# A loop of its own for the memory attention: new order of turns, scores, rounding, outputs and filling products

## What is computed

```python
def memory_cross_attention(u, mem_n, w_mq, w_mkv, w_mo):
    q = (u @ w_mq).reshape(B, S, MEM_HEADS, MEM_HEAD_DIM)        # 4 heads of 256
    k, v = jnp.split(mem_n @ w_mkv, 2, axis=-1)                  # 256 memory tokens
    s = jnp.einsum('bshd,bnhd->bhsn', q, k) * (MEM_HEAD_DIM ** -0.5)
    p = jax.nn.softmax(s, axis=-1)
    o = jnp.einsum('bhsn,bnhd->bshd', p, v).reshape(B, S, D_MODEL)
    return o @ w_mo
```

## Time and profile before

| what | value |
|---|---|
| three runs, median | 1203.12 us |
| the profiled execution | 1202.4 us |
| its span, first to last instruction | 1200.7 us |
| TensorE matmuls busy | 1162.8 us (97% of the span), x5565 |
| VectorE, ScalarE, GpSimd busy | 355.6, 445.9, 472.7 us |
| mean granted clock of TensorE | 0.994 |
| first scores of the memory attention | 724.06 us |
| first matmul behind the last head's outputs | 790.07 us |

### The profile page before, as it was taken

How to read it: one execution, slowest core, us unless ns; L and a number is a source line. 1 busy time by engine, 2 the same in 40 slices (tenths; PEclk the granted TensorE clock), 3 DMA queues, 4 the chain that set the end, 5 groups by cost and what they waited for, 6 DMA issues and landing times.

```text
span 1200.7 us, 14983 instructions
## 1 busy us (share of the span) xinstructions
PE 1162.8 (97%) x5565; PEld 963.0 (80%) x5565; DVE 355.6 (30%) x713; ACT 445.9 (37%) x728; POOL 472.7 (39%) x216
## 2 busy tenths in 40 slices
PE   8999999999999999999899999799999999999998
PEld 6888888888888778788678878678888888888886
DVE  3131221310006264655546104516213122130003
ACT  5232232322126455454535534425523223232213
POOL 2344354354442542222224753122543434435441
PEclk9999999999999999999999999899999999999999
DMA  6232323232322222111223442022332333323233
GB/s 197 88 105 87 105 87 105 88 105 88 105 90 69 88 88 71 53 53 54 71 70 117 146 142 88 18 71 71 93 101 94 98 97 95 100 93 104 90 102 109
DMA packets 83835, 110.91 MB, mean 92 GB/s; under 512 B 8718, under 2 KB 53836, under 8 KB 83788
## 3 DMA queue, kind: packets, MB, share of 16 engines
q1 hardware_dynamic: 83696, 110.24, 28.1%
q10 hardware_dynamic: 92, 0.02, 0.0%
HBM read 108.14 MB, written 2.10 MB: 92 GB/s over the span
## 4 chain that ended last, share of the span: by engine, by line
PE 67%; issue 19%; POOL 8%; DVE 4%; ACT 1%; DMA 1%; SPq 0%; POOLq 0%; DVEq 0%; ACTq 0%
PE bank L1397 22%; PE bank L1401 22%; PE bank L1398 22%; POOL w_lo L566 7%; DVE h L1050 1%; DVE tmp L1039 1%; DMA raw<-in_ffn_w_gu 1%; ACT w_hi L622 0%; POOL q_hi L604 0%; POOL q_lo L604 0%; DVE pt_lo L1170 0%; DVE xl L1002 0%; PE bank L1418 0%; PE bank L1421 0%; DVE smax L1144 0%
## 5 line engine op out<-in xcount | busy, mean ns | idle before, releaser
L566 POOL TENSOR_TENSOR w_lo<-raw,w_hi 128x1024 fp32r<-128x1024 f32 x193 | 461.5, 2403 | 707.5 <-ACT w_hi L622 695.2
L1397 PE MATMUL bank<-xh,w_hi 128*128 128x512 f32 (+1 forms) x920 | 353.3, 384 | 5.2 <-POOL w_lo L566 2.6
L1401 PE MATMUL bank<-xl,w_hi 128*128 128x512 f32 (+1 forms) x920 | 351.8, 382 | 0.0
L1398 PE MATMUL bank<-xh,w_lo 128*128 128x512 f32 (+1 forms) x920 | 351.7, 382 | 0.0
L622 ACT ACTIVATE w_hi<-raw 128x1024 fp32r<-128x1024 f32 x196 | 204.5, 1056 | 361.3 <-DMA raw<-in_ffn_w_down 169.3
L1397 PEld LDWEIGHTS bank<-xh,w_hi 128*128 128x128 f32 x920 | 173.0, 188 | 40.3 <-issue 3.9
L1401 PEld LDWEIGHTS bank<-xl,w_hi 128*128 128x128 f32 x920 | 173.1, 188 | 33.9
L1398 PEld LDWEIGHTS bank<-xh,w_lo 128*128 128x128 f32 x920 | 173.2, 188 | 32.2
L1397 PE MATMUL bank<-w_hi,mid_hi 128*128 128x512 f32 x352 | 137.3, 390 | 0.0
L1398 PE MATMUL bank<-w_hi,mid_lo 128*128 128x512 f32 x352 | 137.0, 389 | 0.0
L1401 PE MATMUL bank<-w_lo,mid_hi 128*128 128x512 f32 x352 | 137.0, 389 | 0.0
(11 more groups left out here) (227 smaller groups left out, 1168.6 us busy)
## 6 DMA issues: line engine op xcount, KB each, us to landing
raw<-in_ffn_w_gu SPq DMA_DIRECT2D x176, 256.0 KB, 2.9
raw<-in_ffn_w_down SPq DMA_DIRECT2D x88, 256.0 KB, 2.8
raw<-in_mix_w_in SPq DMA_DIRECT2D x48, 256.0 KB, 2.8
raw<-in_mem_w_kv SPq DMA_DIRECT2D x32, 256.0 KB, 3.1
raw<-in_mix_w_out SPq DMA_DIRECT2D x16, 256.0 KB, 2.8
raw<-in_mem_w_q SPq DMA_DIRECT2D x16, 256.0 KB, 3.0
raw<-in_mem_w_o SPq DMA_DIRECT2D x16, 256.0 KB, 2.9
h<-in_x SPq DMA_DIRECT2D x4, 512.0 KB, 5.3
```

Of the source, the lines that this page charges most:

```text
L566: gp.tensor_tensor(w_lo[:, n % SLOTS, :], raw[:, n % SLOTS, :], w_hi[:, n % SLOTS, :].bitcast(F32), ALU.subtract).then_inc(lo_ready, 1)
L1397: pe.matmul(dst, w[0], x[0], start=start, stop=False, skip_group_check=loose)
L1398: pe.matmul(dst, w[1], x[0], start=False, stop=False, skip_group_check=loose)
L1401: return pe.matmul(dst, w[0], x[1], start=False, stop=stop, skip_group_check=loose)
```

## The change

The loops for FoX and for the memory attention are parted on ScalarE and VectorE (`fox_attention`, `mem_attention`) and on TensorE. FoX's order stays as it was. In the memory attention:

- TensorE turns unit k-2 first in the iteration, ahead of the filling and of `scores(k)`. A head's outputs come in iteration k for unit k-2 (before: for k-3), so there are 18 iterations, and the first two quarters still stand before the first scores.
- ScalarE rounds unit k-2's turned rows ahead of exponential k. `round_to` moves to the end of the iteration, behind the output copies. The two output copies have the copy-out of the query chunks between them.
- VectorE makes unit k-2's low part first, then maximum k, `normalise(k-1)`, and the output copies. `mq_lo` stands in the same iteration as `mq_hi` (before: one later).
- The filling ends one iteration earlier: three quarters in iterations 3 and 4, one in iterations 6 and 7. The first pair of chunks is complete in iteration 5 (before: 6), the last in iteration 7 (before: 8).

```diff
-EARLY_OUT = ((0,), (1,), ())
+EARLY_OUT = ((0,), (1,))
-MEM_FILL = ((2, 0), (1, 1), (1, 1), (1, 1), (1, 1), (1, 1), (1, 1), (0, 1), (0, 1))
+MEM_FILL = ((2, 0), (1, 1), (1, 1), (1, 2), (1, 2), (1, 1), (0, 1), (0, 1))
...
             def mem_attention():          # ScalarE
...
+                for k in range(N_MEM + LATE):
+                    if k >= LATE:
+                        turned_hi(k - LATE)
+                    if k < N_MEM:
+                        exponent(k)
+                    ended = k >= LATE and MEM_UNITS[k - LATE][1] == TC - 1
+                    if ended:
+                        output(MEM_UNITS[k - LATE][0], 0)
+                    if k == MEM_PAIR_TURN:
+                        mq_hi(1, (0, 1))
+                    if ended:
+                        output(MEM_UNITS[k - LATE][0], 1)
+                    if k == len(MEM_FILL) - 1:
+                        mq_hi(1, (2, 3))
+                    round_to(mem_block("q", 1, 0) + 3 + MEM_FILLED[min(k, len(MEM_FILL))] // 4
+                             + (k > len(MEM_FILL)))
...
             def mem_attention():          # VectorE
...
+                for k in range(N_MEM + LATE):
+                    if k >= LATE:
+                        turned_lo(MEM, k - LATE)
+                    if k < N_MEM:
+                        dve.wait_ge(scored, u + 1)
...                                        # maximum, scaled maximum: as before
+                    if 1 <= k <= N_MEM:
+                        normalise(N_FOX + k - 1, NMEM)
+                    if ended:
+                        output(MEM_UNITS[k - LATE][0], 0)
+                    if k == MEM_PAIR_TURN:
+                        mq_lo(1, (0, 1))
+                    if ended:
+                        output(MEM_UNITS[k - LATE][0], 1)
+                    if k == len(MEM_FILL) - 1:
+                        mq_lo(1, (2, 3))
...
-                for k in range(len(units) + late + 1):          # TensorE
-                    mem_fill(filled, before)
-                    scores(k)
-                    first_output(EARLY_OUT[k - len(units)])
-                    output(k - late - 1, 0)
-                    mem_fill(filled + before, after)
-                    output(k - late - 1, 1)
-                    turn(k - late)
+                    for k in range(N_MEM + LATE):
+                        if k >= LATE:
+                            turn(k - LATE)
+                        mem_fill(filled, before)
+                        if k < N_MEM:
+                            scores(k)
+                        else:
+                            first_output(EARLY_OUT[k - N_MEM])
+                        output(k - LATE, 0)
+                        mem_fill(filled + before, after)
+                        output(k - LATE, 1)
```

More of the change, by code:

```diff
@@ L804, in cum_spread, with fox_attention @@
                 act.activation(cum_b[:, hd % 2, :], bank[cum_slot(hd) % 2][:, :], ACT.Copy).then_inc(cb_ready, 1)
-            def attention(phase):
-                units, u0, late, mem = UNITS[phase], FIRST_UNIT[phase], LATE, phase != FOX
+            def fox_attention():
                 def output(done):
-                    if not 0 <= done < len(units) or units[done][1] < TC - 1:
+                    if not 0 <= done < N_FOX or FOX_UNITS[done][1] < TC - 1:
                         return
[L813 to L824, removed]
-                        cum_spread(k // TC + 1)
[L826 to L840, removed]
-                        round_to(B_IN + KB * FILL_GROUPS[0] + 2 + sum(FILL[:k]) // 4)
[L842 to L854, removed]
-                                       ACT.Copy).then_inc(pt_h, 1)
[L856 to L867, removed]
@@ L935, in mixer @@
                 in_evacuate(2, (2, 3))
-                attention(FOX)
+                fox_attention()
                 gla()
@@ L964, in memory @@
                 act.wait_ge(hinv, 3)
-                attention(MEM)
+                mem_attention()
                 round_to(B_UP2)
@@ L1137, in attention @@
-                for k in range(len(units) + late + 2):
-                    if k < len(units):
-                        u, w = u0 + k, key_width(mem, units[k][1])
+                    hd = FOX_UNITS[done][0]
+                    r = slice(FOX_D * (hd % 2), FOX_D * (hd % 2 + 1))
+                    dve.wait_ge(y_h, hd + 1)
+                    dve.tensor_tensor(fox_lo[r, hd // 2, :], o_bank(FOX, hd)[r, :], fox_hi[r, hd // 2, :].bitcast(F32),
+                                      ALU.subtract).then_inc(y_l, 1)
@@ new lines, in fox_attention @@
+                for k in range(N_FOX + LATE + 2):
+                    if k < N_FOX:
+                        hd, i = FOX_UNITS[k]
+                        w, r = key_width(False, i), slice(k % 4, k % 4 + 1)
+                        dve.wait_ge(scored, k + 1)
+                        if i == 0:
+                            dve.wait_ge(cb_ready, hd + 1)
+                        if k >= PROBS:
+                            dve.wait_ge(pturned, k - PROBS + 1)
+                        dve.tensor_tensor_reduce(prob[:, k % PROBS, 0:w], s_bank(FOX, k)[:, 0:w],
+                                                 cum_b[:, hd % 2, 0:w], -1.0, -NEG, ALU.add, ALU.min,
+                                                 accum_out=nmx[:, r]).then_inc(maxed, 1)
+                    if 1 <= k <= N_FOX:
+                        normalise(k - 1, key_width(False, FOX_UNITS[k - 1][1]))
+                    if k == 0:
+                        in_evacuate(2, (2, 3))
+                    if k == 2:
+                        in_evacuate(1, (), (2, 3))
+                    if 0 <= k - LATE < N_FOX:
+                        turned_lo(FOX, k - LATE)
+                    output(k - LATE - 1)
+                    for g in (3, 5):
+                        if k == PAIR_TURN[g - 3]:
+                            in_evacuate(g, (0, 1))
+                        if k == END_TURN[g - 3]:
+                            in_evacuate(g, (2, 3))
+                    if 0 < k - END_TURN[0] <= 3:
+                        decayed(k - END_TURN[0] - 1)
@@ L1158, in attention @@
[L1158 to L1168, removed]
-                        dve.wait_ge(pt_h, u0 + k - late + 1)
-                        dve.tensor_tensor(pt_lo[:, js, i * P:(i + 1) * P],
-                                          p_bank(phase, k - late)[:, 0:nk * P].rearrange("p (j n) -> p j n", n=P),
-                                          pt_hi[:, js, i * P:(i + 1) * P].bitcast(F32),
-                                          ALU.subtract).then_inc(pt_l, 1)
@@ L1698, in output @@
                     last.then_inc(pv_done, 1)
-                for k in range(len(units) + late + 1):
-                    before, after = MEM_FILL[k] if mem and k < len(MEM_FILL) else (0, 0)
-                    filled = MEM_FILLED[k] if k < len(MEM_FILL) else 0
-                    mem_fill(filled, before)
-                    if k < len(units):
-                        scores(k)
-                    if phase == FOX:
-                        fill(k)
-                    if mem and k >= len(units):
-                        first_output(EARLY_OUT[k - len(units)])
-                    output(k - late - 1, 0)
-                    mem_fill(filled + before, after)
-                    if mem:
-                        output(k - late - 1, 1)
-                    if 0 <= k - late < len(units):
-                        turn(k - late)
+                if mem:
+                    for k in range(N_MEM + LATE):
+                        before, after = MEM_FILL[k] if k < len(MEM_FILL) else (0, 0)
+                        filled = MEM_FILLED[k] if k < len(MEM_FILL) else 0
+                        if k >= LATE:
[8 more added lines that the diff above has]
+                        output(k - LATE, 1)
+                    return
+                for k in range(N_FOX + LATE + 1):
+                    if k < N_FOX:
+                        scores(k)
+                    fill(k)
+                    output(k - LATE - 1, 0)
+                    if 0 <= k - LATE < N_FOX:
+                        turn(k - LATE)
             def first_output(ms):
```

121 lines of the change are left out of this document (76 added, 45 removed).

## The result

The changed kernel is slower: 1210.32 us in the median of 4 runs (1209.93 to 1211.19) against 1203.18 us before; ratio 1.0057, 95% interval [1.0041, 1.0073]. I had forecast 1205.0 us in a range of 1199.8 to 1208.2, "no change" with 0.67; the third rival, slower through half clock, said 1208.5. The forecast was wrong. Of all launches reported here one, of e2_psum_exp, took 3014 us, at a granted clock of 1.0; it is left out of that kernel's median and interval.

What follows compares the result with a forecast made beforehand. TensorE, busy 97% of the span, was taken to bound the kernel, so only its stalls and slow clock could go. Order +0.3 and half clock +2.1 gave +2.4 us on 1202.4: 1204.8, stated as 1205.0, range 1199.8 to 1208.2.

Steps and rivals of the forecast that it cites:

- no change: Whole kernel: a measured time within about 0.3%, 3.6 us, of the time before; chance 0.67.
- the third rival: Between 767 and 787, thinly filled iterations pull the clock down again and again: +6.1 us, 1208.5; chance 0.16.
- The order, iteration by iteration: Memory attention, worked through to head 3's outputs: at full clock throughout, the change ends 0.3 us later.
- behind an output copy: Iteration 14: the output copy stands in front of the high part, without rounding; the iteration takes 2.95 us.
- over two outputs: Iteration 13: 1.38 us to the output and 2.84 for both outputs, 4.22 us in all.
- stalls before turns 5, 7 and 9: TensorE waits before turning units 5, 7 and 9, in iterations 7, 9 and 11: 1.3, 2.6 and 2.6 us.
- wait for query chunks: The 2.5 us wait before scores 8 goes in name; its copies still hold up the turn.
- The clock: Memory attention: half clock behind the two 2.6 us stalls, before iterations 9 and 11, costs 2.1 us.
- Two stretches of half clock: Outputs of head 1, 1.4 to 1.6 us, and the plain iteration 11, whose scores are delayed by 0.7.
- its upper bound: Four remaining stretches between 771 and 787 at half clock too: 0.7 for three plain ones, 1.6 for outputs, 3.7 us more.
- Rival 2: Memory attention: the new loop doesn't bind, turns stay 2.00 us apart; -4.2 us, 1198.5; chance 0.14.
- The signs that I had named: Wrong if TensorE's stalls sum under 8 or over 18 us, iteration 5 waits for GpSimd's split, or stage end moves outside 0-5 us.

Runs made afterwards that it cites:

- e2_psum_exp: The changed kernel with the memory attention's exponentials left in their PSUM bank, so VectorE's normalising reads PSUM and writes SBUF; median 1209.21 us.
- e3: The changed kernel with TensorE's turn of unit k-2 put behind the scores of k, except where it closes a head; median 1206.78 us.
- e4: The changed kernel with roundings moved on ScalarE: blocks 0 and 1 behind exponential 4, block 2 behind 9, block 3 behind 13; median 1205.14 us.

## Why the prediction was wrong

- **The order, iteration by iteration: right.** At held clock the stage is 65.05 us; the working gave 787.56 - 724.06 = 63.5, and with the 1.62 us of the port 65.1. Turns at 2.42 and 2.41 (said 2.43), 2.94 behind an output copy (2.95), 4.23 over two outputs (4.22). The stage after has the stalls before turns 5, 7 and 9 (1.9, 2.4, 3.3 us; said 1.3, 2.6, 2.6), and the wait for query chunks is gone in name, as said.
- **The clock: mis-sized, and this is the step that failed.** "I take 2.1 us": it was 4.9. Two stretches of half clock were allowed for, on the outputs of head 1 (1.4) and on iteration 11 (0.7); the trace has 0.52 and 0.59 us there. The stretches behind them, between 771 and 787, I put at nothing in the sum, though I had named them as its upper bound. They took 0.76 us in iteration 12, 1.49 in 13 and 1.56 in 16, 3.8 us in all. The 3.7 us that I had named for them is what came, but the range did not reach that far. I treated the clock as a matter of single long stalls. Over the plain iterations, with stalls of 1.2 us between short groups of matmuls, it stayed down for 10 us. That was the third rival (0.16), and its test, a clock below 0.8 over 765:785, is met with 0.74. Its 1208.5 is 1.8 us short, about the long rows of the next point. In reading the kernel before I had also counted three shorter stalls behind the 2.15 us one that left the clock alone; the trace has four (0.93, 0.79, 1.75 and 1.13 us).
- **The port: missing.** 1.62 us stood in none of the terms. The sum of 0.33 + 1.62 + 4.92 us gives 6.87 of the 6.91 measured. Neither miss alone would have left the range: 1205.0 with the 2.8 us of clock is 1207.8, with the 1.6 us of the port 1206.6, with both 1209.4. In the memory attention of the kernel before the same instruction was never above 0.45 us, because its roundings stood where the splits missed it or met it only in their last 0.3 us; moving `round_to` moved the splits onto it. I had followed `round_to` through ScalarE's queue, and asked of GpSimd only whether the weights came in time.
- **Rival 2 was right about what is possible, not about this kernel**: in the changed kernel it takes VectorE's low part behind the normalising for turns to come under 2.1 us apart (1.37).
- **The signs that I had named.** One sign of being wrong came: the first matmul behind the last head's outputs starts at 797.58 us, 7.5 us later than before, where I had allowed 0 to 5. TensorE's stalls of 13.1 us lie within 8 to 18, and no wait for GpSimd's split appeared.
- What stays open: why half clock fell on one stretch rather than another in kernels with like stalls (e2, e3, e4). The runs show that it goes when TensorE is kept at work, in three pairs of kernels: the stage of the profiled executions falls by 5.0, 4.1 and 2.4 us, the medians against their own before by 3.2, 4.6 and 2.9.

## What to carry to other kernels

When two queues hand work back and forth, write the loop with its lags: an operation that needs this iteration's product, put first in its queue, makes everything behind it wait, while last in its queue it has an iteration of slack. A moved instruction moves what it releases: look at what runs beside the released work, on shared ports too. Where thin iterations follow one another, price half clock over the whole stretch and not only behind the longest stalls, and try a few dummy matmuls in the stalls; here they gave back 2.9 to 4.6 us by the medians. Before crediting an edit with a gain in one profile, check that the gain lies behind the edit: here 2.27 of 4.15 us did not.

## What I had not expected of the hardware

A VectorE multiply by a column, 128x256 float32 from SBUF to SBUF, takes 0.35 us alone and up to 2.15 us when GpSimd's 2.4 us subtraction runs; the same multiply with its input in PSUM takes 0.48 us with or without it. In FoX's attention of the kernel before, rows of this line were held up as well (a 128x512 one took 1.71 us where others took 0.49, a 128x128 one 1.15 where others took 0.29): the sign was there to be read.
